# Input and output projection of the 32 sample tokens in four 32-column groups of the array

## What is computed

```python
z = x @ w_in                      # (tokens, 1024) @ (1024, 3252), columns go to head groups
ya = dsa_attend(...)              # top-256 (sample: top-72) keys by an indexer, softmax over them
ob, s_new = gla(...)              # gated linear attention, chunked
hc, c_new, n_new, m_new = mlstm(...)
y = concat(ya, yb, yc) @ w_out    # (tokens, 1024) @ (1024, 1024)
x = layer_norm(ALPHA * x + y)
x = layer_norm(ALPHA * x + moe(x))   # 16 experts, top 2 of one group
```

## Time and profile before

| | |
|---|---|
| time, median of 3 runs | 1520.9 us (1512.1 to 1523.42) |
| span of the profiled execution | 1520.2 us |
| what the profiled execution took outside its span | not given |
| PE busy, share of the span | 1318.4 us, 87% |
| DVE busy | 775.7 us, 51% |
| ACT busy | 398.4 us, 26% |
| input projection, all tiles, line 1188 | 450.6 us in 1152 MATMULs |
| output projection, all tiles, line 1282 | 131.2 us in 288 MATMULs |
| mean granted clock of TensorE | 0.88 of full speed |

### The profile page before, as it was taken

One profiled execution on the slowest core, in us unless ns is written; L12 is line 12 of the kernel. 1 busy time (PEld: TensorE's weight loads), 2 busy tenths in 40 slices (PEclk: granted clock), 3 DMA queues, 4 the chain that ended last, 5 costly groups with the idle time before them and its releaser, 6 DMA issues. The chain is left out here.

```text
span 1520.2 us, 16147 instructions
## 1 busy us (share of the span) xinstructions
PE 1318.4 (87%) x5597; PEld 813.6 (54%) x5597; DVE 775.7 (51%) x1787; ACT 398.4 (26%) x805; POOL 431.7 (28%) x460
## 2 busy tenths in 40 slices
PE   5898899999999999999898997996289999999800
PEld 2566565755656656656654544653156666666500
DVE  0024125778778878988897988333300000000078
ACT  1142424324324224224314212311011111111111
POOL 5103024052151251261055012002231111113487
PEclk9999899999999898999898988575679999999955
DMA  8966645536543443443333333001078766667163
GB/s 272 313 200 210 231 145 179 173 108 201 155 159 123 146 147 112 146 147 108 113 113 122 110 94 118 1 14 29 4 252 301 235 218 234 211 203 250 35 221 121
DMA packets 146265, 238.60 MB, mean 157 GB/s; under 512 B 17211, under 2 KB 117474, under 8 KB 146194
## 3 DMA queue, kind: packets, MB, share of 16 engines
q1 hardware_dynamic: 131298, 197.66, 40.3%
q0 software_dynamic: 10064, 29.16, 5.9%
q10 hardware_dynamic: 4832, 10.88, 2.3%
HBM read 211.38 MB, written 26.29 MB: 156 GB/s over the span
## 5 line engine op out<-in xcount | busy, mean ns | idle before, releaser
L1188 PE MATMUL bank_pair<-win,xT 128*128 128x384 f32 (+7 forms) x1152 | 450.6, 542 | 14.8 <-DMA win<-in_w_in 13.7
L1188 PEld LDWEIGHTS bank_pair<-win,xT 128*128 128x128 f32 (+1 forms) x1152 | 213.3, 193 | 192.0 <-issue 100.9
L897 DVE MAX8 top<-score 128x8 f32<-128x384 f32 (+6 forms) x201 | 174.9, 870 | 4.0
L898 DVE MATCH_REPLACE8 score<-top,score 128x384 f32<-128x384 f32 (+6 forms) x201 | 171.9, 855 | 0.0
L1282 PE MATMUL bank_pair<-w_out,yT 128*128 128x512 f32 (+1 forms) x288 | 131.2, 610 | 0.4 <-ACT yT L623 0.4
L1641 DVE COPY rows<-bank_pair 32x1024 f32<-32x1024 f32 x16 | 19.4, 1212 | 170.3 <-PE bank_pair L1677 170.3
L567 POOL TENSOR_TENSOR small<-small,pexp 128x4 f32<-128x4 f32 (+1 forms) x9 | 9.4, 1049 | 335.9 <-DVE small L1078 335.9
L1677 PE MATMUL bank_pair<-wd,hT 128*128 128x512 f32 (+1 forms) x192 | 98.8, 653 | 0.0
L1551 POOL DMA_INDIRECT xg<-x_rows,ids x32 | 30.1, 941 | 229.1 <-PE bank_pair L1656 215.9
L1282 PEld LDWEIGHTS bank_pair<-w_out,yT 128*128 128x128 f32 (+1 forms) x288 | 52.8, 186 | 74.0 <-issue 72.2
L1142 PE MATMUL bank_pair<-ident,lm 128*128 128x128 f32 (+2 forms) x234 | 43.2, 312 | 45.8 <-ACT lm L733 15.8
(11 more groups left out here) (339 smaller groups left out, 2091.7 us busy)
## 6 DMA issues: line engine op xcount, KB each, us to landing
win<-in_w_in SPq DMA_DIRECT2D x90, 768.0 KB, 4.4
win<-in_w_in SPq DMA_DIRECT2D x18, 1024.0 KB, 5.3
win<-in_w_in SPq DMA_DIRECT2D x18, 840.0 KB, 5.2
win<-in_w_in SPq DMA_DIRECT2D x18, 800.0 KB, 4.6
wg<-in_w_exp_gate SPq DMA_DIRECT2D x12, 1024.0 KB, 6.2
wu<-in_w_exp_up SPq DMA_DIRECT2D x12, 1024.0 KB, 9.4
wd<-in_w_exp_down SPq DMA_DIRECT2D x12, 1024.0 KB, 11.1
expert_rows<-rows ACTq DMA_DIRECT2D x16, 512.0 KB, 3.3
```

What stands on the lines that cost most here:

```text
L897: step(V.max(top8[0:n], sc))
L898: step(V.match_replace(sc, top8[0:n], sc, NEG))
L1188: last = mmul(zb[0:n, 0:w], xT[:, kk, 0:n], win[:, i % NWIN, k, 0:w], start=(kk == 0), stop=(kk == KD - 1))
```

## The change

For the sample tile alone (t = 8) both projections use the array as four groups of 32 columns. Group q holds the same 128 x 32 block of activations as weights (each group loads it for itself) and streams its own quarter of the output columns; the result stands on partitions 32q to 32q+31 of the bank, in the first quarter of its columns. A new function `pieces(j)` gives the four ranges of a cut: quarters, but for cut 1 (420 wide) three of 128 and one of 36. ACT copies each quarter from its partitions to partitions 0 to 31 (`side_by_side`): four copies where there was one, for cut 1 five where there were four. The output projection issues all of its work in slot 12, with one raise of `wo_ps`, and slot 13 has nothing on PE; DVE adds the residual in four pieces of 256 columns after that one signal. The other tiles are as before. No DMA transfer, buffer or slot is added or moved.

```diff
--- before.py
+++ after.py
@@ -51,6 +51,13 @@
 CUTS = [0, 512, 932, 1316, 1700, 2100, 2484, 2868, P_IN]
 NCUT = len(CUTS) - 1
 WCUT = max(b - a for a, b in zip(CUTS, CUTS[1:]))
+
+
+def pieces(j):
+
+    w = CUTS[j + 1] - CUTS[j]
+    p = 128 if j == 1 else w // 4
+    return [(p * c, min(p * c + p, w)) for c in range(4)]
 
 
 def tokens(t):
@@ -638,6 +645,29 @@
                 act.wait_ge(S("ln0_scale"), t + 1)
                 A.activation(xt, xt, ACT.Identity, bias=sm(tokens(t), NB0), scale=sm(tokens(t), RSTD0)).then_inc(S("x_normed"), 1)
 
+            def side_by_side(j, t, zb):
+
+                zp = [zb[SMP * c:SMP * c + SMP, 0:hi - lo] for c, (lo, hi) in enumerate(pieces(j))]
+                n, out = SMP, []
+                if j == 1:
+                    out += [(va[0:n, t, 128 * c:128 * c + 128], zp[c]) for c in range(2)]
+                    out += [(zix[0:n, 0:128], zp[2]),
+                            (zix[0:n, 128:256].rearrange("p (h d) -> p h d", h=H), zp[3][:, 0:DI].unsqueeze(1).to_broadcast([n, H, DI])),
+                            (zw[0:n, t % 2, :], zp[3][:, DI:DI + H])]
+                    return out
+                for c, (lo, hi) in enumerate(pieces(j)):
+                    dst = {
+                        0: lambda: zqk[0:n, lo:hi],
+                        2: lambda: zg[0:n, c // 2, 2 * (c % 2):2 * (c % 2) + 2, 0:DK],
+                        3: lambda: zv[0:n, t % 2, lo:hi],
+                        4: lambda: zr[0:n, lo:hi],
+                        5: lambda: zc[0:n, lo:hi],
+                        6: lambda: zm[0:n, t % 2, c, 0:HC],
+                        7: lambda: zo[0:n, lo:hi],
+                    }[j]()
+                    out.append((dst, zp[c].rearrange("p (h d) -> p h d", h=2) if j == 2 else zp[c]))
+                return out
+
             def cut(t, c):
                 n, j, i = tokens(t), ORDER[c], use(t, "cut", c)
                 w = CUTS[j + 1] - CUTS[j]
@@ -651,6 +681,9 @@
                                     2: [("qk_ready", t)], 3: [("gla_o_ps", t - 1)] if t > 1 else [],
                                     6: [("ml_s_ps", t - 1)] if t > 1 else []}.get(j, []):
                         act.wait_ge(S(name), v)
+                if t == NPT:
+                    evacuate(i, side_by_side(j, t, zbank(i)))
+                    return
                 evacuate(i, {
                     0: lambda: [(zqk[0:n], zp)],
                     1: lambda: [(va[0:n, t, :], zp[:, 0:WA]), (zix[0:n, 0:128], zp[:, WA:WA + 128]),
@@ -926,7 +959,12 @@
                            sm(n, AINV, H).unsqueeze(2).to_broadcast([n, H, HA]), ALU.mult).then_inc(S("ya_ready"), 1)
                     if s == 13:
                         dve.wait_ge(S("x0_back"), 16 * (t + 1))
-                        for c in range(2):
+                        for c in range(4) if t == NPT else ():
+                            dve.wait_ge(S("wo_ps"), 2 * t + 1)
+                            cs = slice(256 * c, 256 * c + 256)
+                            tell(STT(out=x1[0:n, cs], in0=x1[0:n, cs], scalar=ALPHA, in1=SC[SMP * c:SMP * c + SMP, 0:256],
+                                     op0=ALU.mult, op1=ALU.add), "residual_done", 2 * t + c + 1)
+                        for c in range(2) if t < NPT else ():
                             dve.wait_ge(S("wo_ps"), 2 * t + c + 1)
                             cs = slice(512 * c, 512 * c + 512)
                             tell(STT(out=x1[0:n, cs], in0=x1[0:n, cs], scalar=ALPHA, in1=SC[0:n, cs],
@@ -1183,7 +1221,13 @@
                         u = use(t, "cut", c)
                         zb = zbank(u) if half % 2 else bank(u)
                         pe.wait_ge(S(f"win_loaded{i % NWIN}"), 16 * (i // NWIN + 1))
-                        for k in range(4):
+                        if t == NPT:
+                            for k in range(4):
+                                kk = 4 * (half % 2) + k
+                                for q, (lo, hi) in enumerate(pieces(ORDER[c])):
+                                    last = mmul(zb[SMP * q:SMP * q + SMP, 0:hi - lo], xT[:, kk, 0:n], win[:, i % NWIN, k, lo:hi],
+                                                start=(kk == 0), stop=(kk == KD - 1))
+                        for k in range(4) if t < NPT else ():
                             kk = 4 * (half % 2) + k
                             last = mmul(zb[0:n, 0:w], xT[:, kk, 0:n], win[:, i % NWIN, k, 0:w], start=(kk == 0), stop=(kk == KD - 1))
                         last.then_inc(S("p_ps") if half % 2 else S("half_cuts"), 1)
@@ -1278,12 +1322,21 @@
                                 pe.wait_ge(S("w_out_loaded"), 16)
                             pe.wait_ge(S("yT_ready"), 2 * t + 2)
                             pe.wait_ge(S("lm_ready"), H * (t + 1))
+                        if t == NPT:
+                            for k in range(KD) if c == 0 else ():
+                                for q in range(4):
+                                    last = mmul(SC[SMP * q:SMP * q + SMP, 0:256], yT[:, k, 0:n], w_out[:, k, 256 * q:256 * q + 256],
+                                                start=(k == 0), stop=(k == KD - 1))
+                            if c == 0:
+                                last.then_inc(S("wo_ps"), 1)
+                            yield
+                            continue
                         for k in range(KD):
                             last = mmul(SC[0:n, 512 * c:512 * c + 512], yT[:, k, 0:n], w_out[:, k, 512 * c:512 * c + 512],
                                         start=(k == 0), stop=(k == KD - 1))
                         last.then_inc(S("wo_ps"), 1)
                     if s == 17:
-                        pe.wait_ge(S("wo_ps"), 2 * t + 2)
+                        pe.wait_ge(S("wo_ps"), 2 * t + (2 if t < NPT else 1))
                         for g in range(2):
                             pe.wait_ge(S(("x1_left", "x1_right")[g]), t + 1)
                             four(x1[0:n], n, g).then_inc(S("x1T_ps"), 1)
```

## The result

The changed kernel takes 1505.2 us (median of 20 runs, 1494.0 to 1514.3) against 1516.9 for the kernel before, run in turn with it on the same chip. The ratio is 0.9925, with a 95% interval of 0.9902 to 0.9948: a gain of 11.4 us, between 7.9 and 14.9. One of the 20 runs of the kernel before took 1745.9 us, in a slower state of the chip, and is not in the ratio. Forecast were 1514 us and a gain of 7. The time lies in the range of 1503 to 1529, near its low end, and outside the forecast's own range of 1510 to 1518. About 4 of the 9 us between forecast and result are the base: the kernel before was at 1520.9 in the runs known then, and at 1516.9 here. The rest is a gain that is larger than forecast.

What follows compares the result with a forecast made beforehand. Taken as bounds: DVE in pass 7, PE at a low clock in pass 8, the bare chain in pass 9. Pass 9's -8.9 us and pass 7's +2 gave -7, from 1520.9 to 1514 us; 8-in-10 range 1503 to 1529.

Steps and rivals of the forecast that it cites:

- What bounds each pass: DVE sets pass 7's length, PE at a low clock bounds pass 8, a bare chain through PE bounds pass 9.
- The term of -10.0: Pass 9, sample's output projection on PE: four groups streaming together take 5.2 us instead of 15.23, saving 10.0 us.
- The bound for two at a time: Pass 9, output projection: if only two groups overlap, 32 steps take 8.6 us, saving 6.6.
- the third rival: Both projections: weight loads not covered (+9 us, 1530) or groups not overlapping (about +2); chance 10%.
- the drain at a change of tiling mode: Array on PE: a skill page says changing tiling mode drains it; the prediction saw no room for that in eight earlier passes.
- DVE's four pieces: Pass 9, residual addition after the output projection: four pieces take 1.76 us instead of 0.70, +1.1 us on the chain.
- ACT's 22 further copies: Pass 7, input projection: at most 11 us more on ACT, which is idle for 91 of 128 us.
- The input projection: Pass 7: between -3 us with the clock as before and +8 to +10 with it low; taken as +2.
- rival 1: Pass 7: the clock stays up, -3.2 us there, -12 us in all, 1509 us; chance 22%.
- PE is 6.9 us later: Pass 7, up to the logits DVE wants at 853.86: with a low clock throughout, PE is 2.7 us beyond its slack.
- the most that can be won: Pass 7: DVE can use only 3.2 us, its two waits for PE, of PE's freed 25 to 40.
- Rival 2: Pass 7: clock low until 896 us, +8 to +10 there, 1521 in all, or 1531 with two groups at a time; chance 20%.

Runs made afterwards that it cites:

- out_only: Kernel before with only the output projection in four groups, input projection as before: ratio 0.9943 to before, 4.94 us on PE for the output projection.
- in_only: Kernel before with only the input projection in four groups, output projection as before: ratio 0.9987 to before, pass 7 125.4 us.
- wout_three: Changed kernel with the sample's output projection computed three times over in place: 18.0 us on PE for that stage, one profiled execution.
- two_groups: Changed kernel with the sample's output projection in two groups of 512 columns instead of four of 256: 8.38 us on PE, one profiled execution.
- by_group: Changed kernel with the output projection's eight contraction blocks of one group done before the next group: 12.89 us for the stage, one profiled execution.
- experts_too: Changed kernel plus the 32 overflow rows of each expert's down projection in four groups: 1455.4 us, ratio 0.9623 to before.
- full_2: The changed kernel again, unaltered, in a later series on another chip: 1498.5 us, ratio 0.9896 to before.
- full: The changed kernel again, unaltered, run beside the two halves of the change: ratio 0.9893 to before.
- warm: Changed kernel with 12 idle full-width array passes added on PE in pass 9, results unused: ratio 0.9972 to before.

## Why the prediction was right or wrong, point by point

**What bounds each pass: right.** DVE in pass 7, the bare chain in pass 9. `out_only` and `in_only` show it: 21.9 instead of 53.5 us of PE make pass 7 shorter by 1.8 us, and 4.94 instead of 15.23 make the later stretch shorter by 9.2, which is their difference less the 1.1 of DVE's additions.

**The output projection: right, and in this pair 1.2 us off by the clock.** The 0.43 us step of four abreast is in the rows of the loads, the 0.21 one in `wout_three`. 5.2 us were forecast with a rise of the clock after 3.1 us; in after it came after some 5.6 us, which makes 5.6/0.43 = 13 steps slow, 3 fast (0.64) and the tail: 6.4. Six other profiles have 4.88, 4.94, 4.99, 5.21, 5.41 and 6.42. The term of -10.0 was -8.85 in this pair and is -10.3 where the clock rises at the same place before and after. That it does so after an edit was the weak part of it. The bound for two at a time, 8.6, was 8.38 in `two_groups`; what I had not seen is how much the overlap hangs on the order (12.89 us in `by_group`). The changed kernel issues its groups in turn.

**Weight loads and the third rival: it fell.** A list in the page "TensorE: Matmul & The Clock Gate" of the Trainium skill (Part 3, The mechanism) lets a load overlap only if the row group differs; the paragraph above it in the same section also names loads to a background weight buffer. Here all four groups have the same rows, and 64 loads of 32 columns disappear behind the streams: 4 passes with their loads take 0.43 us at the low clock, and in `wout_three` 0.21 at the full one. So the list's "only" does not hold here; which buffer the loads went to no trace shows. "TensorEngine Tiling (Array Packing)" (Key Properties) states that tiles can load and multiply in parallel; with that the trace agrees, as long as neighbours go to different tiles.

The prediction also read the earlier trace rows against the drain at a change of tiling mode. Those eight passes change the tile and not the mode, so they say nothing on it. Where 128-column and 32-column weights alternate, in `experts_too` at the full clock, the starts at a change lie 0.53 us apart for a stream of 0.43, and 0.33 for one of 0.21: 0.1 us for each change. In `full_2`, with the same alternation and no tiles, it is 0.52 for 0.43. So there is a price, a small one, and it is not new with the tiles.

**DVE's four pieces: right.** 1.76 us forecast and measured, in all profiles with four pieces. ACT's 22 further copies cost 4.0 us (398.4 to 402.4), where I had bounded them by 11; DVE waited for none of them, and PE for 0.7 us in all, behind two.

**The input projection: the sign was wrong, by 2 to 4 us.** Forecast were +2, measured -1.8 in after and in `in_only`, -0.4 in `full`. The premise held: the clock fell, to 0.70 between 815 and 896 us, so rival 1 (it stays up, -3.2) is wrong in its mechanism. That the gain of 11.4 is near its -12, nearer than to the forecast, is luck. The step that failed is "PE is 6.9 us later". It set every logits group, every value group and the rest at the low clock. PE's timeline in after:

```profile
817.67 1.77 PE L1269 MATMUL bank_pair<-kT,qT 64*128 64x512 f32 x4
819.37 1.08 PE L1228 MATMUL bank_pair<-win,xT 128*32 128x128 f32 x32
821.69 0.88 PE L1295 MATMUL bank_pair<-va,pT 128*128 128x64 f32 x6 [1.24 <-ACT pT L630]
824.14 1.11 PE L1180 MATMUL bank_pair<-ident,lm 128*128 128x128 f32 x4 [1.56 <-ACT lm L766]
...
831.41 3.35 PE L1269 MATMUL bank_pair<-kT,qT 64*128 64x512 f32 x4
...
838.35 1.93 PE L1228 MATMUL bank_pair<-win,xT 128*32 128x128 f32 x32
...
845.37 1.77 PE L1269 MATMUL bank_pair<-kT,qT 64*128 64x512 f32 x4
```

PE ends the third logits group at 847.14, 35.6 us after DVE began the pass; before it was 849.67, 36.9 us after. So PE is 1.3 us earlier there, not 6.9 later. One logits group of three is slow, and it takes 3.35 us: 1.6 us more instead of 6 for all three. The 3.78 of the earlier trace rows was the wrong price, since that row is not the same work: the logits of pass 8 have 1024 keys (two MATMULs of 512 columns, each twice), those of pass 7 have 896 (512 and 384, as the order of instructions shows). With 1024 keys the full clock takes 1.98 us (at 931.12 in the kernel before), so a group of 896 gets 1.6 us longer by the low clock and not 2.0. The clock falls at about 823 us, where PE has run ahead and waits for ACT (the 1.24 and 1.56 us above), and is back by 840. What it then costs comes out of time that PE had won.

It doesn't always go so. Nine profiles have the tiled input projection of after. In five of them (after, `in_only`, `wout_three`, `warm`, `experts_too`) the clock rises 4.6 us into pass 7, the first logits take 1.77 us and the pass 125.3 or 125.4. In the other four (`full`, `full_2`, `by_group`, `two_groups`) it is low through the first and the second logits, 3.35 us each, and the pass takes 126.8. In `full` PE then ends the third logits at 832.41, 37.0 us after DVE's start, 0.2 later than before: the sample's five halves are 9.2 us shorter, as forecast, the two slow logits 3.2 longer, the five value groups 3.0, the rest some 3 instead of 6.4. So even there the term of 6.9 is 0.2. Why the first rise comes or stays out is open; the kernel before and `out_only` both have it.

The waits of DVE in pass 7 show what came of it; after, then before (us in total, times, longest):

```profile
DVE small L1092 <- ACT small L842: 2.8, 1, 2.8
DVE gtmp L1050 <- PE bank_pair L1388: 1.9, 1, 1.9
DVE small L1115 <- ACT gtmp L849: 1.5, 1, 1.5
```

```profile
DVE qcT L1094 <- PE bank_pair L1435: 1.7, 1, 1.7
DVE lm L918 <- PE bank_pair L1225: 1.5, 1, 1.5
...
DVE small L1077 <- ACT gtmp L816: 0.5, 1, 0.5
```

The two waits for PE of the earlier trace rows are gone, 3.2 us; 1.0 comes back as a longer wait for ACT (the third row of after, the last of before). In both kernels that instruction of ACT had itself waited for PE (13.0 and 8.4 us), so it is PE again that is late next, one engine removed. That leaves 2.2, of which 1.8 are seen in the length of the pass. I had called 3.2 the most that can be won and should have asked who is late next. In `full`, with the slow first logits, DVE has this wait besides:

```profile
DVE lm L951 <- issue: 1.7, 1, 1.7
```

The profile names no releaser, but PE's logits end at 805.97 and DVE's row begins at 806.11. The 126.8 us of these four profiles are the worst that was seen, and still no loss. Rival 2 (+8 to +10 in this pass) is out.

**DMA: covered, as said.** The last halves now wait for their weights:

```profile
914.86 1.15 PE L1228 MATMUL bank_pair<-win,xT 128*32 128x96 f32 x32 [3.26 <-DMA win<-in_w_in]
```

3.26 us on PE, and none of DVE's waits is behind it.

**The sum.** By stretches of the profiles -7.8 and -1.8 are from the edits, -9.6, where -8.9 and +2 were forecast; another -1.0 ahead of the output projection and -0.6 behind the barrier are not assigned. The measured gain of 11.4 (7.9 to 14.9) holds either sum. So the forecast of -7 was off by 2.6 us in its terms only because two errors partly cancel: 1.1 us too much for the output projection, by the late rise of the clock, and 3.8 too little for the input projection. The base of three runs was 4.0 us above the median of 20. With the 16.2 and 15.8 us of `full` and `full_2` the gain may be some us larger than the stretches explain.

## What to carry to other kernels

If the stationary operand has 32 columns, give each of four column groups a quarter of the moving columns and issue the groups in turn, block by block: here PE then took 0.41 and 0.42 of its time for the two projections, loads and all (0.32 for the output projection where the clock rose at the same place), and 0.34 in the experts. Do it first where PE is the bound or stands alone on the chain (40 us in the experts, 8 in pass 9), not where it feeds another engine (0.4 or 1.8 us for 32 us of PE). A term at a low clock should be priced from a row of the same shape, and from where PE will be early, not as if the low clock held throughout.

## What was not expected of the hardware

- Groups overlap in full only if neighbours in the order of issue go to different ones: 4.88 to 6.42 us in turn, 12.89 group by group. At each change of group four passes of the next start beside the last four of the one before.
- The same code has its clock rise 2.5 to 3.6 us into the output projection in eight profiles and about 5.5 us into it in four, tiled or not; that is 1.4 us of PE.
- A run of 192 short passes stood still for 1.49 and 0.58 us after 125 of them, with no release to wait for in the profile, and the clock was low afterwards for 3.4 us. Why, and whether the one caused the other, is open.
- Reading PSUM from partitions 32q on and writing to partitions 0 to 31 cost DVE 0.44 us for 256 columns, for each of the four groups alike (1.76 for four).
- With the same program up to there, the start of pass 7 lay between 795.4 and 815.2 us over twelve profiles.
